# Reading page numbers ahead, unrolling the rotary-key loads and moving the second sample group between the heads of a latent-attention step

## The chip, the core and the metric

The kernel runs on one core of one Trainium2 chip. The metric is the time of one execution on the device in microseconds. Three runs of the kernel before gave 940.86 us as their median (938.93 to 948.01). Engines are named as the profile names them: PE is TensorE (matmuls), DVE is VectorE, ACT is ScalarE, POOL is GpSimd, and SP is SyncE, which computes nothing and issues most of the transfers.

## The reference, cut to what matters

The reference is one inference step of a decoder with two layers, for a prompt of 256 tokens and a sample group of 8 sequences with one new token each, all in float32 with a model width of 1024. Layer 0 mixes tokens with a causal convolution, layer 1 with multi-head latent attention; behind each mixer stand a mixture of 32 experts (two per token) and a gated embedding, and at the end a norm.

The change lies in the attention of layer 1. Each of the 8 sample sequences has 1024 past positions in a paged cache. A page table of 8 times 8 integers says which pages of the pool are a sequence's own:

```
def latent_attend(q_lat, q_pe, c_kv, k_pe, mask):
    s = (einsum('bqhl,bkl->bhqk', q_lat, c_kv)
         + einsum('bqhr,bkr->bhqk', q_pe, k_pe)) * ATTN_SCALE
    p = softmax(where(mask, s, -inf))
    return einsum('bhqk,bkl->bqhl', p, c_kv)

def gather_past(j):
    ckv = cache_ckv[page_table, j].reshape(n_seq, -1, KV_LORA)      # 8 x 1024 x 256
    kpe = cache_kpe[page_table, j].reshape(n_seq, -1, QK_ROPE_DIM)  # 8 x 1024 x 32
```

There are 16 heads. The prompt attends to itself with keys and values expanded per head; the samples attend in the latent space, to the cache and to their own new token.

## The kernel before, in words

The program is written by hand for each engine: five instruction streams, each in the order of its own block, and semaphores between them. Nothing reorders an engine's work, so what stands behind a wait waits as well. Matmul results go to 8 banks of PSUM taken in turn (`open_bank`); `arrive` waits until a bank's result is there, `freed` until a bank has been read out.

**Weights and the ring.** Weights come in pieces of 1 MB through a ring of 9 slots, filled by SP in a fixed order (`fill`, `load_expert`); piece g waits for the last use of piece g minus 9 (`used_up`, table `last`). Between the experts of layer 0 (`expert_stream(0)`) and those of layer 1 (`expert_stream(1)`) SP issues 16 pieces: 4 of the gated embedding (from G_PG0), 2 of the query compression (G_DQ), 2 of the key compression (G_DKV), 3 that expand the queries (G_UQ to G_UQ+2), 1 for the keys (G_UK), 1 for the values (G_UV) and 3 of the 4 of the output projection (G_WO). The last one of the output projection is issued behind the cache loads.

**Cache pages.** The 8 sample sequences are two groups of 4 (SB = 4), called group 0 and group 1. A page's latent rows are 256 KB (128 partitions, the rows and their transpose beside each other); 32 pages are one group, 8.4 MB. SP issues one transfer per page (`load_cache`, line 1933). Sequences 0 and 1 of a group go into `page0` (in the arena) and `page1` (in `xn_sq`), sequences 2 and 3 into four ring slots, free once the query expansion is through (SP waits for bank ("qn", 7)). Group 1 goes to the same places, so it waits for group 0's last use, bank ("sv", 0). Each page's number has to be in a register of the issuing engine first: `page_numbers` reads 8 of them with `value_load`, 32 for a group, and SP does so in front of each group's transfers, behind the waits for "kpe" and "kv". The rotary keys of a page are 16 KB; POOL issues their transfers in `load_kpe` (lines 1853 to 1860), 4 loops of 8 turns for a group, and each turn reads one page number (line 1857) and issues one transfer (line 1859). Group 1's rotary keys go to the place of group 0's (`KPT`), so POOL waits for bank ("ss", 0, 1), the second of the three score banks of group 0, before it begins. Between the two groups POOL issues four stores of outputs (lines 1873 to 1877).

**The heads and the sample groups.** PE runs a loop over i = 0 to 18. Step i computes the scores of head i (line 848), for odd i up to 11 the keys of two heads to come (line 483), turns the softmax weights of head i - 2 (line 856), and for even i from 4 the values of two heads (line 870). DVE and ACT run loops of the same steps (maximum, exponential, normalising, copying out). A sample group has four parts on PE: `sample_scores` (line 892, waits for the group's latent rows in `s_ckin` and rotary keys in `s_kpin`), `sample_weights` (lines 901 and 905), `sample_values` (lines 914 and 916, fills bank ("sv", B)) and `sample_out` (line 922). DVE has `sample_max`, `sample_new`, `sample_turned`, `sample_rows` and `sample_latent`, and ACT `sample_exp`. Group 0's four parts stand at the ends of PE's steps i in SAMPLE_AT = [3, 5, 7, 9]; DVE's and ACT's parts are tied to the same numbers. Group 1 stands behind the whole loop on all three engines. Behind both come the samples' values of all heads ("so", line 949) and the output projection "wo" (line 483 again), with which layer 1 goes on to its norm, its router (line 544), its experts (line 623) and the rest.

Of the kernel before, what the change touches and what calls it, by code (L numbers as in the profile page):

```python
# [17 lines left out]
TP, TS = 256, 8  # L18
# [16 lines left out]
H, DN, DR, DV = 16, 64, 32, 64  # L35
QL, KL = 384, 256
KQ, KK = QL // P, KL // P
PAGES, PAGE = 8, 128
PAST = PAGES * PAGE
SB = 4  # L40
# [32 lines left out]
UW = 288  # L73
SW = (TQ - 1) * NQ + TP
PAIRS = KD // 2
SAMPLE_AT = [3, 5, 7, 9]
HK = DN + DR


# [26 lines left out]
G_PG0 = G_MOE0 + NMOE  # L106
# [57 lines left out]
def build(nc, a, out):  # L164
    NPOOL = a["cache_ckv"].shape[0]

    with ExitStack() as ctx:
# [227 lines left out]
        def arrive(eng, key):  # L395

            b, u = taken[key]
            eng.wait_ge(full[b], u + 1)
            return bank[b]
# [59 lines left out]
        def _(pe):  # L459
# [436 lines left out]
            def sample_weights(B):  # L896
                pe.wait_ge(t_pe, B + 1)
                for hf in range(2):
                    ps = open_bank(pe, ("sp", B, hf))
                    for g in range(4):  # L900
                        t = tr(ps[:, g * P:(g + 1) * P], pp[:, (4 * hf + g) * P:(4 * hf + g + 1) * P], ident)
                    t.then_inc(is_full(("sp", B, hf)), 1)
                ps = open_bank(pe, ("sn", B))
                pe.wait_ge(t_pn, B + 1)
                tr(ps[0:TS, 0:P], pnew, ident).then_inc(is_full(("sn", B)), 1)
# [19 lines left out]
            for i in range(H + 3):  # L925
                if i < H:
                    scores(i)
                if i % 2 == 1 and i // 2 + 2 < KD:
                    keys(i // 2 + 2)
                if i == 1:  # L930
                    turn_queries()
                if 2 <= i < H + 2:
                    turn_weights(i - 2)
                if i >= 4 and i % 2 == 0:
                    values(i // 2 - 2)

                if i in SAMPLE_AT:
                    (sample_scores, sample_weights, sample_values, sample_out)[SAMPLE_AT.index(i)](0)
            sample_scores(1)
            sample_weights(1)  # L940
            sample_values(1)
            sample_out(1)
            ps = open_bank(pe, "so")
            for B in range(TS // SB):
                freed(pe, ("st", B))
# [26 lines left out]
        def _(dve):  # L972
# [549 lines left out]
            for i in range(H + 2):  # L1522
                if i < H:
                    head_max(i)
                if 1 <= i <= H:
                    head_norm(i - 1)
                if i == 1:
                    queries_in()
                if i >= 5 and i % 2 == 1:
                    head_out((i - 5) // 2)  # L1530
                if i == SAMPLE_AT[1]:
                    sample_new(0)
                if i - 1 in SAMPLE_AT:
                    (sample_max, sample_turned, sample_rows, sample_latent)[SAMPLE_AT.index(i - 1)](0)
            for c in range(KD):
                if (H + 1 - 5) // 2 < c:
                    head_out(c)
            sample_max(1)
            sample_new(1)
            sample_turned(1)  # L1540
            sample_rows(1)
            sample_latent(1)
            ps = arrive(dve, "so")
            v.tensor_copy(oT[:, :, TP:T], ps[:, 0:KD * TS].rearrange("p (c b) -> p c b", c=KD))\
# [10 lines left out]
        def _(act):  # L1555
# [227 lines left out]
            for i in range(H + 2):  # L1783
                if i % 2 == 1 and i // 2 + 2 < KD:
                    keys_in(i // 2 + 2)
                if i < H:
                    head_exp(i)
                if i >= 2:
                    head_weights(i - 2)
                if i == SAMPLE_AT[0] + 1:  # L1790
                    sample_exp(0)
            sample_exp(1)
            squares("n4", hT, KD, h_ready(("wo",)))
            root("n4")
            act.wait_ge(s_done, 32 + 64)
# [12 lines left out]
        def _(pool):  # L1808
# [41 lines left out]
                                           expert_weights(l, e, c)).then_inc(x_w[l], 16)  # L1850
                        pool.wait_ge(x_dn[l], w + 1)

            def load_kpe(B):

                for i in range(SB):
                    with pool.Fori(0, PAGES) as n:  # L1856
                        pg = pool.value_load(pages[0:1, bass.ds(n + (SB * B + i) * PAGES, 1)], min_val=0,  # L1857
                                             max_val=NPOOL - 1)
                        pool.dma_start(KPT[DR * i:DR * (i + 1), bass.ds(n * PAGE, PAGE)],  # L1859
                                       a["cache_kpeT"][bass.ds(pg, 1)].rearrange("o p f -> p (o f)"))\  # L1860
                            .then_inc(s_kpin, 16)

            moe(0)
            pool.wait_ge(s_add, KD * NGR)
            pool.wait_ge(s_pg, 16)
            pool.dma_start(wukT, a["ukT"]).then_inc(s_uk, 16)
            arrive(pool, "kpe")
            g.memset(qlat, 0.0).then_inc(s_qz, 1)
            g.memset(qps, 0.0).then_inc(s_qz, 1)
            g.memset(qsT[:, KD:KD + 3, :], 0.0).then_inc(s_qz, 1)  # L1870
            load_kpe(0)
            pool.wait_ge(s_ck, KK)
            pool.dma_start(out["ckv_p"], ckvT[:, :, 0:TP]).then_inc(s_done, 16)
            pool.dma_start(out["ckv_s"], ckvT[:, :, TP:T]).then_inc(s_done, 16)
# [1 line left out]
            pool.dma_start(out["kpe_p"], kpeT[0:DR, 0:TP]).then_inc(s_done, 16)  # L1876
            pool.dma_start(out["kpe_s"], kpeT[0:DR, TP:T]).then_inc(s_done, 16)
            arrive(pool, ("ss", 0, 1))
            load_kpe(1)
            moe(1)  # L1880

        @block.sync
        def _(sp):
# [93 lines left out]
                for g in range(NSLOT + 2 * p, min(NSLOT + 2 * p + 2, G_MOE0)):  # L1977
                    fill(g)
            expert_stream(0)
            for g in range(G_PG0, G_PIN1 - 1):  # L1980
                fill(g)
            sp.wait_ge(s_pg, 16)
            arrive(sp, "kpe")
            arrive(sp, "kv")
            for B in range(TS // SB):
                numbers = [page_numbers(SB * B + i) for i in range(SB)]
                for i in range(SB):
                    load_cache(SB * B + i, numbers[i])
            for g in range(G_PIN1 - 1, G_MOE1):
                fill(g)  # L1990
            expert_stream(1)
# [94 lines left out]
```

## Time and profile before

| | us |
|---|---|
| median of three runs | 940.86 |
| the three runs | 938.93, 940.86, 948.01 |
| the profiled execution's own time | 949.18 |
| its span in the profile | 947.2 |
| PE busy | 783.3 (83% of the span) |
| PE weight load busy | 566.7 (60%) |
| DVE busy | 319.4 (34%) |
| ACT busy | 206.6 (22%) |
| POOL busy | 56.0 (6%) |
| HBM read | 261.05 MB, 278 GB/s over the span |

The profiled execution took 8.3 us longer than the median of the three runs, of which the slowest took 948.01 us. Its span starts with the first instruction that the profiler shows and ends with the last. Busy shares are means over a program with stages of different kinds; in the two expert stages the transfer engines are saturated at 415 to 419 GB/s, in the attention stage neither they nor PE are busy all the time. The granted clock is TensorE's, as a share of its full 2.4 GHz.

### The profile page before, as it was taken

Reading aid. Unit: us, or ns where it says so; the run is one execution under the profiler, and the core shown is the slowest. Engines: PE = TensorE matmul, PEld = TensorE weight load, DVE = VectorE, ACT = ScalarE, POOL = GpSimd, SP = SyncE. Lnnn points to the kernel's source line nnn. Section 1 sums busy time; section 2 is a strip of 40 time slices with the busy share of each in tenths; the row PEclk is TensorE's granted clock in tenths of the full one; section 3 lists DMA queues with packets and bytes.
Section 4 is the critical chain, followed back from the end, with each engine's and each line's share of the span. In section 5 each row is a group of like instructions: output and inputs, shape, how many; then the busy total and the mean of one; then the engine's idle time right before and its main releaser. Section 6 shows DMA issues by size and latency. Waiting matters only on the chain.

```text
span 947.2 us, 16693 instructions
## 1 busy us (share of the span) xinstructions
PE 783.3 (83%) x6434; PEld 566.7 (60%) x6434; DVE 319.4 (34%) x948; ACT 206.6 (22%) x490; POOL 56.0 (6%) x95
## 2 busy tenths in 40 slices
PE   5999789998777796989997685798997687778894
PEld 4876468765544464667774362588765355445683
DVE  2332134433221331255265271226233132213435
ACT  2100132512111111132135251015311111111222
POOL 5100000000000000000033232000000000000000
PEclk9999889999988988999999796799999898899997
DMA  9853716599999999974319074468699999999501
GB/s 376 300 174 79 249 51 256 191 420 406 415 417 416 415 418 417 418 292 145 122 60 358 22 236 140 171 229 321 270 399 419 415 418 415 418 416 415 225 1 46
DMA packets 59613, 269.32 MB, mean 284 GB/s; under 512 B 7312, under 2 KB 12704, under 8 KB 38416
## 3 DMA queue, kind: packets, MB, share of 16 engines
q1 hardware_dynamic: 53232, 259.37, 69.0%
q10 hardware_dynamic: 3712, 5.35, 1.9%
q0 software_dynamic: 2592, 3.54, 1.3%
q8 instruction: 53, 0.87, 0.4%
q14 instruction: 24, 0.20, 0.1%
HBM read 261.05 MB, written 2.52 MB: 278 GB/s over the span
## 4 chain that ended last, share of the span: by engine, by line
PE 53%; DMA 23%; issue 13%; POOLq 4%; DVE 3%; ACT 1%; ACTq 1%; POOL 1%; SPq 0%; DVEq 0%
DMA ring<-in_moe_w_up 22%; PE bank L483 16%; PE bank L623 15%; PE bank L602 5%; POOLq L1857 3%; PE bank L649 3%; PE bank L664 3%; PE bank L507 3%; PE bank L892 2%; DMA ring<-in_stream 1%; PE bank L558 1%; PE bank L544 1%; PE bank L467 1%; POOLq L1859 1%; POOLq L1856 1%
## 5 line engine op out<-in xcount | busy, mean ns | idle before, releaser
L623 PE MATMUL bank<-ring,arena 128*32 128x256 f32 x2048 | 148.1, 436 | 63.5 <-DMA ring<-in_moe_w_up 61.2
L623 PEld LDWEIGHTS bank<-ring,arena 128*32 128x32 f32 x2048 | 86.8, 125 | 130.3 <-issue 108.1
L483 PE MATMUL bank<-xn_sq,ring 128*128 128x264 f32 x480 | 110.3, 392 | 10.9 <-DMA ring<-in_stream 10.9
L483 PE MATMUL bank<-arena,ring 128*128 128x264 f32 (+1 forms) x456 | 109.6, 401 | 6.5 <-ACT arena L1597 4.0
L483 PEld LDWEIGHTS bank<-xn_sq,ring 128*128 128x128 f32 x480 | 92.5, 193 | 27.8 <-issue 11.7
L1229 DVE TENSOR_TENSOR arena<-arena,bank 128x128 f32<-128x128 f32 x34 | 9.8, 288 | 288.4 <-ACT arena L1638 288.4
L483 PEld LDWEIGHTS bank<-arena,ring 128*128 128x128 f32 x456 | 90.3, 199 | 23.7 <-issue 7.0
L602 PEld LDWEIGHTS bank<-arena 128*128 128x128 f32 x864 | 97.9, 192 | 9.4 <-issue 9.4
L602 PE MATMUL bank<-arena 128*128 128x128 f32 (+1 forms) x864 | 101.1, 277 | 2.0 <-DVE arena L1199 2.0
L649 PE MATMUL bank<-ring,arena 128*32 128x512 f32 x512 | 65.4, 598 | 16.6 <-ACT arena L1645 16.5
L664 PE MATMUL bank<-arena 128*128 128x264 f32 (+1 forms) x288 | 70.5, 399 | 4.7 <-ACT arena L1654 4.7
L664 PEld LDWEIGHTS bank<-arena 128*128 128x128 f32 (+1 forms) x288 | 54.0, 192 | 21.3 <-ACT arena L1654 6.9
L1246 DVE TENSOR_TENSOR hT<-hT,bank 128x264 f32<-128x264 f32 x144 | 61.7, 429 | 13.3 <-PE bank L664 11.1
L1654 ACT COPY arena<-bank 64x512 f32<-64x512 f32 x68 | 39.4, 580 | 76.6 <-PE bank L649 75.8
L1638 ACT ACTIVATE arena<-bank 128x128 f32<-128x128 f32 x34 | 9.4, 277 | 166.5 <-PE bank L623 166.5
L649 PEld LDWEIGHTS bank<-ring,arena 128*32 128x32 f32 x512 | 14.9, 109 | 44.3 <-ACT arena L1645 24.3
L1859 POOL DMA_DIRECT2D arena<-in_cache_kpeT x64 | 32.1, 501 | 71.9 <-issue 71.9
L507 PE MATMUL bank<-arena 128*32 128x256 f32 x512 | 31.3, 406 | 4.5 <-DMA arena<-arena 4.5
L1565 ACT ACTIVATE xn_sq<-hT 128x264 f32<-128x264 f32 x40 | 16.1, 420 | 74.3 <-DVE hT L1000 66.6
L892 PE MATMUL bank<-arena 128*32 128x512 f32 (+1 forms) x96 | 15.4, 468 | 19.7 <-DMA arena<-in_cache_kpeT 19.7
L1630 ACT COPY arena<-bank 128x512 f32<-128x512 f32 (+1 forms) x18 | 10.1, 561 | 94.1 <-PE bank L602 94.1
L507 PEld LDWEIGHTS bank<-arena 128*32 128x32 f32 x512 | 17.0, 117 | 18.3 <-DMA arena<-arena 4.9
(243 smaller groups left out, 790.2 us busy)
## 6 DMA issues: line engine op xcount, KB each, us to landing
ring<-in_moe_w_gate SPq DMA_DIRECT2D x60, 1024.0 KB, 14.0
ring<-in_moe_w_up SPq DMA_DIRECT2D x60, 1024.0 KB, 10.7
ring<-in_moe_w_down SPq DMA_DIRECT2D x60, 1024.0 KB, 12.9
ring<-in_stream SPq DMA_DIRECT2D x35, 1024.0 KB, 12.5
ring<-in_cache_ckv SPq DMA_DIRECT2D x32, 256.0 KB, 7.6
arena<-in_moe_w_down SPq DMA_DIRECT2D x4, 1024.0 KB, 13.3
arena<-in_cache_ckv SPq DMA_DIRECT2D x16, 256.0 KB, 4.1
xn_sq<-in_cache_ckv SPq DMA_DIRECT2D x16, 256.0 KB, 5.5
```

What stands on the lines that cost most here:

```text
L483: t = mm(ps[:, 0:cols], lhs(k), rhs(k), start=(k == 0), stop=(k == n - 1))
L507: t = mm(ps[CG * b:CG * (b + 1), 0:TP], dg[:, c, TQ * b + q, :], shifted[p % 2][:, b, c % 2, NQ * q:NQ * q + TP], start=(q == 0), stop=(q ...
L602: t = mm(bank[k // 4][:, (k % 4) * n:(k % 4 + 1) * n], XR[:, i, k * P:(k + 1) * P], S[:, j % 2, i, 0:n], start=(i == 0), stop=(i == 2))
L623: t = mm(bank[2 + r][p0:p0 + U, 0:F].rearrange("p (c f) -> p c f", c=2), x, w[i][:, :, k * F + c * P:k * F + (c + 1) * P], start=(k == 0), ...
L649: t = mm(bank[4 + r][p0:p0 + U, :], hidT[:, r, U * (2 * i + c):U * (2 * i + c + 1)], w[i][:, c, h * 512:(h + 1) * 512], start=(c == 0), st ...
L664: mm(bank[CBANK[k % 4]][:, 0:T], O[0:n, j % 2, k * P:(k + 1) * P], gate[0:n, j % 2, :], start=True, stop=True).then_inc(s_cb, 1)
L892: t = mm(ps[HP * i:HP * (i + 1), 0:n], qlat[:, k, b, :] if k < KK else qps[:, b, :], keys, start=(k == 0), stop=(k == KK))
L1246: v.tensor_tensor(hT[:, k, :], hT[:, k, :], bank[CBANK[k % 4]][:, 0:T], ALU.add).then_inc(s_add, 1)
L1565: s.activation(sq[:, at + k, :], src[:, k, :], ACT.Square).then_inc(s_sq, 1)
L1654: s.copy(O[64 * r:64 * r + 64, j % 2, 512 * h:512 * (h + 1)], bank[4 + r][64 * h:64 * h + 64, :])\
L1857: pg = pool.value_load(pages[0:1, bass.ds(n + (SB * B + i) * PAGES, 1)], min_val=0, max_val=NPOOL - 1)
L1859: pool.dma_start(KPT[DR * i:DR * (i + 1), bass.ds(n * PAGE, PAGE)], a["cache_kpeT"][bass.ds(pg, 1)].rearrange("o p f -> p (o f)"))\
```

## The change

Four things are changed, and nothing of what is computed.

1. `SAMPLE_AT` holds a list for each group: group 0 at steps 2, 4, 6, 8 (one step earlier), group 1 at steps 12, 14, 16, 18 instead of behind the loop. DVE's and ACT's parts follow; `sample_latent(1)` alone still stands behind DVE's loop.
2. SP reads group 0's 32 page numbers between the pieces G_UQ and G_UQ+1 of the ring, and group 1's right behind the issue of group 0's transfers.
3. POOL reads group 0's 32 page numbers behind layer 0's experts, in front of its wait for their sums, and group 1's behind the issue of group 0's rotary keys, in front of the four stores.
4. POOL issues the rotary keys of a group as 32 transfers written out, with the numbers in registers, instead of 4 loops of 8 turns.

```diff
-SAMPLE_AT = [3, 5, 7, 9]
+SAMPLE_AT = [[2, 4, 6, 8], [12, 14, 16, 18]]
@@ PE
-                if i in SAMPLE_AT:
-                    (sample_scores, sample_weights, sample_values, sample_out)[SAMPLE_AT.index(i)](0)
-            sample_scores(1)
-            sample_weights(1)
-            sample_values(1)
-            sample_out(1)
+                for B in range(TS // SB):
+                    if i in SAMPLE_AT[B]:
+                        (sample_scores, sample_weights, sample_values, sample_out)[SAMPLE_AT[B].index(i)](B)
@@ DVE
-                if i == SAMPLE_AT[1]:
-                    sample_new(0)
-                if i - 1 in SAMPLE_AT:
-                    (sample_max, sample_turned, sample_rows, sample_latent)[SAMPLE_AT.index(i - 1)](0)
+                for B in range(TS // SB):
+                    if i == SAMPLE_AT[B][1]:
+                        sample_new(B)
+                    if i - 1 in SAMPLE_AT[B]:
+                        (sample_max, sample_turned, sample_rows, sample_latent)[SAMPLE_AT[B].index(i - 1)](B)
...
-            sample_max(1)
-            sample_new(1)
-            sample_turned(1)
-            sample_rows(1)
             sample_latent(1)
@@ ACT
-                if i == SAMPLE_AT[0] + 1:
-                    sample_exp(0)
-            sample_exp(1)
+                for B in range(TS // SB):
+                    if i == SAMPLE_AT[B][0] + 1:
+                        sample_exp(B)
@@ POOL
-            def load_kpe(B):
+            def page_numbers(B):
+                return [[pool.value_load(pages[0:1, b * PAGES + n:b * PAGES + n + 1], min_val=0, max_val=NPOOL - 1)
+                         for n in range(PAGES)] for b in range(SB * B, SB * (B + 1))]
+
+            def load_kpe(numbers):
                 for i in range(SB):
-                    with pool.Fori(0, PAGES) as n:
-                        pg = pool.value_load(pages[0:1, bass.ds(n + (SB * B + i) * PAGES, 1)], min_val=0,
-                                             max_val=NPOOL - 1)
-                        pool.dma_start(KPT[DR * i:DR * (i + 1), bass.ds(n * PAGE, PAGE)],
-                                       a["cache_kpeT"][bass.ds(pg, 1)].rearrange("o p f -> p (o f)"))\
+                    for n in range(PAGES):
+                        pool.dma_start(KPT[DR * i:DR * (i + 1), n * PAGE:(n + 1) * PAGE],
+                                       a["cache_kpeT"][bass.ds(numbers[i][n], 1)].rearrange("o p f -> p (o f)"))\
                             .then_inc(s_kpin, 16)
             moe(0)
+            pool.wait_ge(s_pg, 16)
+            numbers = page_numbers(0)
             pool.wait_ge(s_add, KD * NGR)
-            pool.wait_ge(s_pg, 16)
             pool.dma_start(wukT, a["ukT"]).then_inc(s_uk, 16)
             arrive(pool, "kpe")
...
-            load_kpe(0)
+            load_kpe(numbers)
+            numbers = page_numbers(1)
             pool.wait_ge(s_ck, KK)
...
             arrive(pool, ("ss", 0, 1))
-            load_kpe(1)
+            load_kpe(numbers)
@@ SP
-            for g in range(G_PG0, G_PIN1 - 1):
+            for g in range(G_PG0, G_UQ + 1):
                 fill(g)
             sp.wait_ge(s_pg, 16)
+            numbers = [page_numbers(i) for i in range(SB)]
+            for g in range(G_UQ + 1, G_PIN1 - 1):
+                fill(g)
             arrive(sp, "kpe")
             arrive(sp, "kv")
             for B in range(TS // SB):
-                numbers = [page_numbers(SB * B + i) for i in range(SB)]
                 for i in range(SB):
                     load_cache(SB * B + i, numbers[i])
+                if B == 0:
+                    numbers = [page_numbers(SB + i) for i in range(SB)]
```

## Rows read from the trace of the kernel before

**Rows 1.** Chain of waits, 480 to 680 us: start, duration, what it went through.
```profile
524.30 1.75 DMA arena<-in_cache_kpeT
526.30 7.67 PE bank L892 x48
...
582.55 1.82 DMA arena<-in_cache_kpeT
584.62 7.53 PE bank L892 x48
...
604.70 0.49 DVE rstd L1510
...
608.58 30.45 PE bank L483 x128
```

**Rows 2.** Timeline of PE: start, duration, instruction, idle before and releaser.
```profile
475.40 2.39 PE L467 MATMUL bank<-xn_sq,cst 128*128 128x264 f32 x10
...
495.20 2.83 PE L483 MATMUL bank<-arena,ring 128*128 128x264 f32 x12
...
512.70 0.52 PE L856 MATMUL bank<-cst,arena 128*128 128x128 f32 x3 [0.49 <-DVE arena L1467]
...
515.00 0.52 PE L856 MATMUL bank<-cst,arena 128*128 128x128 f32 x3 [0.26 <-DVE arena L1467]
...
551.36 0.92 PE L848 MATMUL bank<-arena 96*128 96x128 f32 x4
...
574.15 1.55 PE L870 MATMUL bank<-arena 128*64 128x128 f32 x12 [0.66 <-ACT arena L1767]
```

**Rows 3.** Timeline of POOL, the issues of the rotary keys and the stores.
```profile
477.10 0.52 POOL L1859 DMA_DIRECT2D arena<-in_cache_kpeT  x1 [0.64 <-issue]
...
524.30 0.50 POOL L1859 DMA_DIRECT2D arena<-in_cache_kpeT  x1 [1.01 <-issue]
...
526.65 0.73 POOL L1877 DMA_DIRECT2D out_kpe_s<-arena  x1
535.43 0.50 POOL L1859 DMA_DIRECT2D arena<-in_cache_kpeT  x1 [8.05 <-issue]
```

**Rows 4.** Chain of waits, 503 to 506.5 us, one turn of POOL's loop.
```profile
503.37 0.30 POOLq L1857
...
503.93 0.08 POOLq L1859
...
504.07 0.50 issue
```

**Rows 5.** Timeline of SP's queue: start, length of the stretch, transfers issued.
```profile
401.48 9.22 SPq L1919 DMA_DIRECT2D ring<-in_stream  x4
...
426.35 0.33 SPq L1919 DMA_DIRECT2D ring<-in_stream  x1
...
495.51 4.72 SPq L1933 DMA_DIRECT2D arena<-in_cache_ckv  x8
...
504.71 8.14 SPq L1933 DMA_DIRECT2D ring<-in_cache_ckv  x16
551.61 4.06 SPq L1933 DMA_DIRECT2D arena<-in_cache_ckv  x8
```

**Rows 6.** Stretches: length, busy time of each engine, granted clock, DMA share, GB/s.
```profile
520.00:521.00 1.00, 0.00 (x0) 0.00 (x0) 0.00 (x0) 0.00 (x0) 0.26 (x1) 0.50 0.82 293
...
526.30:534.00 7.70, 7.70 (x72) 2.37 (x72) 0.00 (x0) 0.00 (x0) 1.08 (x3) 0.70 0.12 34
...
577.00:578.00 1.00, 0.00 (x0) 0.00 (x0) 0.00 (x0) 0.00 (x0) 0.00 (x0) 0.50 0.23 78
```

**Rows 7.** Transfers of the rotary keys: duration ns min/median/max on POOL, and landing.
```profile
L1859 POOL DMA_DIRECT2D arena<-in_cache_kpeT x64: 496/496/608, 477.1 to 582.6; - x64
...
DMA to landing us min/median/max: 1.7/3.2/5.5
```

**Rows 8.** Chain of waits, 700 us to the end: the first long transfer waits.
```profile
714.00 9.58 DMA ring<-in_moe_w_up
```

## The prediction

> **What bounds the kernel now.** I began with the chain of waits through the attention stage. The reader is to see that it runs over POOL twice: PE's sample scores start when the last rotary-key transfer of a group has landed, at 526.30 us for group 0 and at 584.62 us for group 1, and the output projection starts at 608.58 us [rows 1]. PE's own timeline says how long it had been ready: its step 3 ends at 515.52, so it stood still for 10.8 us, and its last head work ends at 575.70, so it stood still for 8.9 us [rows 2]. Then the timelines of the two issuing engines. POOL issues group 0's rotary keys from 477.10 to 524.30, 31 intervals of 1.52 us [rows 3], though the transfer instruction itself takes 0.50 us. SP issues group 0's latent rows only from 495.51 [rows 5], though what it waited for (the sums of squares) was over at 475.40 + 2.39 = 477.8 [rows 2]; in the 17.7 us between it reads 32 page numbers, 0.55 us each. Last the stretches of the transfer engines: after those 32 transfers they are busy until about 521, after group 1's until about 577.5 [rows 6]. So the rotary keys end both waits by 3 to 7 us over the latent rows, and what comes behind them is the second group's serial tail, 584.6 to 608.6, in which PE has no heads to do.
>
> Behind the projection the order is fixed by PE until 714, where the expert stream begins to hold it [rows 8]. The stream's pieces wait for ring slots that PE frees in the projection and after, and for the router's order, so I let everything behind "wo" move with its start, one for one.
>
> **SP, group 0.** The page numbers are read behind piece G_UQ, issued at about 410.4, the last of four [rows 5]. 32 x 0.55 = 17.7 us end at 428.4; the piece that follows was issued at 426.35 [rows 5], so it comes 2 us later. Its user is the query expansion after 480 us; the cover is 50 us, and the cost nothing. The first 16 pages then start at 477.8 instead of 495.5. The other 16 wait for the last query bank, full at 495.20 + 2.83 = 498.0 [rows 2]; their issue takes 8.1 us [rows 5]. Landing: 32 pages took from 495.5 to 521, 25.5 us. Sixteen take at least half, 12.8 us, and at most the 8.1 us of issue and the 8 us from the last issue (504.71 + 8.14 = 512.85) to 521 [rows 5, 6]: 510.8 to 514.1. I take 512, as the first half is out of the way by then.
>
> **POOL, group 0.** Reading a number took 503.37 to 503.93, 0.56 us; the address 0.14 us; the issue 0.50 us; the other 0.3 us of a turn are the loop [rows 4]. Reading moves in front of POOL's wait for the sums of layer 0's experts; its 18 us lie beside the last experts, and only the keys' wait at 477 would show them. It costs nothing. Written out, a transfer takes 0.14 + 0.50 = 0.64 to 0.7 us; the last key transfer and the four stores, which stand written out, come 0.59 us apart (524.30 to 526.65) [rows 3]. The bounds are 0.59 and 1.52; I take 0.67, near the rows of the same shape. The 32 are issued by 477.1 + 31 x 0.67 = 497.9 and land up to 5.5 us later [rows 7], at 503.4. They no longer end the wait.
>
> **PE, group 0.** Its scores now stand behind step 2, whose end is 512.70 + 0.52 = 513.2 [rows 2]. DVE's copy of the turned queries ends about then. I take a start of 513.5, 12.8 us earlier (bounds 513.2 and 514.5). They took 7.7 us at a mean granted clock of 0.70 [rows 6], having started at 1.2 GHz after the idle stretch. Without that stretch they need 7.7 x 0.70 = 5.4 us at 2.4 GHz if the clock were all; between 5.4 and 7.7 I take 6.0, near the lower, since PE is busy right up to them. End: 519.5. From there to the end of group 0's values PE does four steps: 526.30 + 7.67 = 533.97 to 551.36, 17.4 us [rows 1, 2]. The four steps of after (3 to 6) have two key chunks and two values like those (4 to 7), so again 17.4: 536.9. Up to this point 14.5 us are gained.
>
> **POOL, group 1.** 32 readings end at 498.6 + 32 x 0.56 = 516.5, the four stores at about 519; the wait for the second score bank ends near 518.5. The cover for the readings is thus just long enough, and if it fell short by 5 us nothing would change: 32 transfers of 0.67 us end at 540.5 and land by 546, 17 us before they are needed (below).
>
> **SP, group 1.** The readings (506.2 to 524) lie under PE's steps; cover 13 us. The transfers start 0.25 us after group 0's values (551.36 to 551.61) and landed 577.5 - 551.6 = 25.9 us later [rows 2, 5, 6]: 536.9 + 0.25 + 25.9 = 563.0. This is the wait that is late next.
>
> **PE, group 1.** Eleven steps from 551.36 to 575.70 are 2.2 us each [rows 2]; six steps bring PE to the end of step 12 at about 550.5. It then stands for 12 us, and with it heads 13 to 15, which are queued behind the wait in order; DVE and ACT have nothing to do in the meantime. As the clock falls in such a stretch, the scores take 7.7 us again: 570.7. Steps 13 to 16 correspond to the 17.4 us, less two key chunks and the scores of a head that doesn't exist; I take 16.0 (bounds 13 and 19, the upper because group 1's work on DVE now queues with the heads'): 586.7. Steps 17 and 18 put one turning and one pair of values ahead of `sample_out`: 2.0 us (bounds 0.5 and 3.1). The rest of the tail, 604.70 to 608.58, is 3.9 us [rows 1]. The projection starts at 592.6.
>
> **Sum.** 608.6 - 592.6 = 16.0 us. The parts: 12.8 + 1.7 before group 0's values, and behind them 0.25 + 25.9 + 7.7 + 16.0 + 5.9 = 55.7 against 57.2 before, 1.5. Against the profiled execution's own 949.2 that gives 933.2 us. This execution was 8.3 us above the median of the three runs; the terms are waits and issues and don't depend on that, so I take them off the median: 940.9 - 16.0 = 924.9, say 925.
>
> **Rivals.**
> *More is gained.* Steps 13 to 18 at their lower bounds (13 + 0.5) and the group's transfers in 23 us: 4.5 + 2.9 more, 917.5. For it: PE has few waits left in heads with no keys to expand. Against: DVE's and ACT's round trip set the 2.2 us.
>
> *Half is gained.* The second half of group 0's pages takes as long as a whole group did because the rotary keys' many small packets share the engines with them: 498 + 22 = 520. Then group 0 starts at 520, 6.5 us later than forecast, at 1.2 GHz and once more 7.7 us long: 16.0 - 6.5 - 1.7 = 7.8 gained, 933. For it: landing of rotary keys stretches from 1.7 to 5.5 us beside the rows [rows 7]. Against: in the forecast the keys are all issued by 498.
>
> *The stream absorbs it.* If the experts' transfers from 714 us on [rows 8] were limited by when their stream began and that didn't move, nothing would be left: 941. Against: its pieces wait for PE's slots.
>
> *Slower: POOL can't issue faster.* The 1.52 us could be what a POOL transfer costs when 32 of them follow each other, whatever stands between. The second group would then decide: reading 32 numbers and the stores (about 21 us) would come between the two sets of transfers. With p us each, group 1's keys land at 477 + 32p + 21 + 32p + 3; with p = 1.52 at 598, PE's scores start there instead of 563, and the projection at 598 + 7.7 + 16 + 5.9 = 627.6, 19 us later than now: 960. It turns slower where the scores start after 579 (592.6 + 16.0 taken back), that is at p = 1.22. For it: no row shows more than five POOL transfers in a row without a loop. Against: those five come 0.59 us apart, and every one of the 64 lasts 0.50 us, at most 0.61 [rows 3, 7].
> The Trainium skill (SBUF — State Buffer, "SBUF: two separate sides") speaks for this rival: POOL's transfer descriptors are written through a port pair that certain DVE copies lock, and a transfer then waits for the copy. By its figures (about 620 ns alone, 3100 ns overlapped) an estimate for each transfer beside such a copy would lie far above 1.22 us. The trace doesn't agree so far: the second 32 were issued while DVE worked on the heads (535 to 576 us), and the longest of all 64 took 0.61 us [rows 7].
>
> **Chances.** Forecast 0.62, with a range of its own of 919 to 931; more 0.10; half 0.14; absorbed 0.06; slower 0.08. About 1%, 9.4 us, is what a measurement of this kernel can tell from no change. Faster by over that: the forecast, more, and half of "half", 0.79. Within: the other half and the absorbed case, 0.13. Slower 0.08. The range takes in the forecast's bounds, "more" in part and "half": 916 to 935.
>
> **What would show it.** In the trace of after: SP's first page at about 478 and its seventeenth at 498; POOL's rotary keys 0.6 to 0.7 us apart; group 0's scores near 513.5 at a high clock, ended by a DVE copy or latent rows and no more by rotary keys; one wait of about 12 us at line 892 near 551 to 563, now on latent rows; "wo" near 592. The prediction is wrong if POOL's intervals stay above 1.2 us, if PE's wait for group 1 is longer than 20 us, if steps 13 to 18 take more than 25 us, or if "wo" moves and the first expert wait near 714 doesn't.

## The result and the profile after

The changed kernel took 932.5 us, the median of 20 runs (925.16 to 938.57), against 945.8 us for 20 runs of the kernel before (938.93 to 954.67). The ratio is 0.987 with a 95% interval of 0.9846 to 0.9893: 10 to 15 us faster. The time lies in the forecast range of 916 to 935 us, though above the 919 to 931 that the forecast had without its rivals; the forecast gain of 16.0 us is a little above the interval.

The profiled execution took 925.16 us, 24.0 less than the 949.18 of before. That is more than the change did, and one has to cut the trace to see it. The query expansion (36 matmuls on line 483), ahead of which PE's code is the same and SP's and POOL's readings are hidden, starts 8.7 us earlier, at 471.72 instead of 480.44 us; in the other traces of this study it starts between 476.6 and 482.8. So I compare **the stretch** from that start to the start of the output projection: 608.58 - 480.44 = 128.1 us before, 588.00 - 471.72 = 116.3 us after, and the same 116.3 in a second profile of the changed kernel. The change is worth 11.9 us there. Each kernel was profiled once and only the changed one twice, so the stretch of one trace is a single reading. Behind the projection 3.4 us differ, of which more below. To set a moment of after beside one of before, add 8.7 us.

The chain of waits of the changed kernel, 470 to 620 us (start, duration, what it went through):

```profile
471.72 26.63 PE bank L483 x104
...
504.60 5.52 PE bank L892 x69
...
523.62 3.59 PE bank L914 x64
527.21 0.64 PE bank L916 x2
528.01 0.34 SPq L1932
...
545.67 8.06 DMA ring<-in_cache_ckv
553.72 0.35 issue
554.08 8.23 PE bank L892 x69
562.30 0.87 PE bank L848 x4
...
576.37 5.42 PE bank L914 x64
581.79 0.62 PE bank L916 x2
...
588.00 31.57 PE bank L483 x128
```

POOL is gone from it, where before it stood twice [rows 1]. Group 0's scores (504.60) follow PE's step 2 with no wait, and do 5.5 us of work, not 7.7 [rows 6]. The one wait left is for latent rows: from the end of group 0's values (527.85) over SP's 32 issues to the landing at 553.7. Behind it, from 562.30 to 582.41, comes what the forecast had too short.

PE's waits, 500 to 620 us (who waited for whom: us in total, times, longest):

```profile
PE bank L892 <- DMA ring<-in_cache_ckv: 11.3, 1, 11.3
PE bank L856 <- DVE arena L1464: 3.8, 7, 1.5
PE bank L870 <- ACT arena L1761: 3.0, 6, 0.7
PE bank L901 <- ACT arena L1775: 2.3, 1, 2.3
```

POOL's timeline, which answers to [rows 3]:

```profile
467.68 7.93 POOL L1856 DMA_DIRECT2D arena<-in_cache_kpeT  x14
476.00 10.34 POOL L1856 DMA_DIRECT2D arena<-in_cache_kpeT  x18 [0.39 <-issue]
504.09 0.70 POOL L1872 DMA_DIRECT2D out_ckv_p<-arena  x1 [17.75 <-issue]
...
505.78 0.73 POOL L1876 DMA_DIRECT2D out_kpe_s<-arena  x1
510.65 18.37 POOL L1856 DMA_DIRECT2D arena<-in_cache_kpeT  x32 [4.13 <-PE bank L892]
```

32 transfers take 18.37 us, 0.574 each instead of 1.52. The 17.75 us in front of the stores are the 32 readings, 0.555 each; behind the stores POOL still waits 4.1 us for group 0's scores, so the readings are hidden.

SP's queue, which answers to [rows 5]:

```profile
469.29 4.35 SPq L1932 DMA_DIRECT2D arena<-in_cache_ckv  x8
473.82 4.49 SPq L1932 DMA_DIRECT2D xn_sq<-in_cache_ckv  x8
489.47 8.78 SPq L1932 DMA_DIRECT2D ring<-in_cache_ckv  x16
528.01 3.95 SPq L1932 DMA_DIRECT2D arena<-in_cache_ckv  x8
```

With 8.7 added the first page goes out at 478.0 and the seventeenth at 498.2. The transfer engines are done with group 0 in the microsecond from 503 (busy share 0.26, and nothing from 504 to 505), about 512 on the scale of before as forecast, and only 1 us ahead of PE's scores: an earlier place for group 0 would soon wait for latent rows. And POOL's transfers of the rotary keys, which answer to [rows 7] (ns min/median/max):

```profile
L1856 POOL DMA_DIRECT2D arena<-in_cache_kpeT x64: 496/496/748, 467.7 to 528.5; - x64
...
DMA to landing us min/median/max: 1.7/2.2/5.6
```

Issued nearly three times as densely, half of them still take 496 ns, and the longest 748. That longest one met DVE's copy of the keys' rotary part, from SBUF to SBUF (POOL's transfers, 477.2 to 477.7 us, and DVE's timeline):

```profile
L1856 POOL DMA_DIRECT2D arena<-in_cache_kpeT x1: 748/748/748, 477.2 to 477.2; - x1
```

```profile
477.38 0.75 DVE L1416 COPY arena<-arena 32x512 f32<-32x512 f32 x2
```

### The profile page after: what moved, and what is told of

Read it like the earlier page. It is cut to its first block, busy times and chain, and to the rows that moved or that the text cites. A ratio compares the mean times of both kernels' runs of the same rounds, so it can differ in the third digit from the quotient of the medians.

```text
span 923.2 us, 16491 instructions
## 1 busy us (share of the span) xinstructions
PE 767.7 (83%) x6434; PEld 558.3 (60%) x6434; DVE 318.5 (35%) x948; ACT 205.8 (22%) x490; POOL 56.1 (6%) x95
## 4 chain that ended last, share of the span: by engine, by line
PE 64%; DMA 25%; DVE 4%; issue 2%; ACT 2%; SPq 2%; ACTq 1%; DVEq 0%
PE bank L483 25%; DMA ring<-in_moe_w_up 23%; PE bank L623 15%; PE bank L602 6%; PE bank L649 3%; PE bank L664 2%; PE bank L507 2%; SPq L1932 1%; PE bank L892 1%; DMA ring<-in_stream 1%; PE bank L914 1%; PE bank L467 1%; PE bank L544 1%; DMA ring<-in_cache_ckv 1%; PE bank L745 1%
## 5 line engine op out<-in xcount | busy, mean ns | idle before, releaser
L623 PE MATMUL bank<-ring,arena 128*32 128x256 f32 x2048 | 143.2, 424 | 67.7 <-DMA ring<-in_moe_w_up 65.3
L623 PEld LDWEIGHTS bank<-ring,arena 128*32 128x32 f32 x2048 | 83.7, 122 | 132.9 <-issue 109.0
L1243 DVE TENSOR_TENSOR hT<-hT,bank 128x264 f32<-128x264 f32 x144 | 61.7, 428 | 12.9 <-PE bank L664 10.8
L649 PEld LDWEIGHTS bank<-ring,arena 128*32 128x32 f32 x512 | 14.8, 109 | 44.3 <-ACT arena L1639 24.3
L1624 ACT COPY arena<-bank 128x512 f32<-128x512 f32 (+1 forms) x18 | 10.1, 562 | 94.1 <-PE bank L602 94.1
L507 PE MATMUL bank<-arena 128*32 128x256 f32 x512 | 28.5, 380 | 1.5 <-DMA arena<-arena 1.5
L1218 DVE COPY arena<-bank 128x512 f32<-128x512 f32 (+1 forms) x18 | 11.9, 661 | 36.9 <-PE bank L602 36.9
L507 PEld LDWEIGHTS bank<-arena 128*32 128x32 f32 x512 | 16.2, 110 | 13.3 <-DMA arena<-arena 1.9
## 6 DMA issues: line engine op xcount, KB each, us to landing
ring<-in_moe_w_down SPq DMA_DIRECT2D x60, 1024.0 KB, 13.3
```

Of the source, the lines that this page charges most:

```text
L507: t = mm(ps[CG * b:CG * (b + 1), 0:TP], dg[:, c, TQ * b + q, :], shifted[p % 2][:, b, c % 2, NQ * q:NQ * q + TP], start=(q == 0), stop=(q ...
L623: t = mm(bank[2 + r][p0:p0 + U, 0:F].rearrange("p (c f) -> p c f", c=2), x, w[i][:, :, k * F + c * P:k * F + (c + 1) * P], start=(k == 0), ...
L649: t = mm(bank[4 + r][p0:p0 + U, :], hidT[:, r, U * (2 * i + c):U * (2 * i + c + 1)], w[i][:, c, h * 512:(h + 1) * 512], start=(c == 0), st ...
L1218: v.tensor_copy(xe[:, j % 2, 0:4, 0:n], bank[0][:, 0:4 * n].rearrange("p (k n) -> p k n", k=4))\
L1243: v.tensor_tensor(hT[:, k, :], hT[:, k, :], bank[CBANK[k % 4]][:, 0:T], ALU.add).then_inc(s_add, 1)
L1624: s.copy(xe[:, j % 2, 4:KD, 0:n], bank[1][:, 0:4 * n].rearrange("p (k n) -> p k n", k=4))\
```

## Experiments

**The changed kernel again, and its parts taken apart.** First the changed kernel without an edit (after_again):

> The changed kernel once more, beside the others of this group on the same chip. I follow one stretch in every trace: from the start of the query expansion (line 483, 36 matmuls) to the start of the output projection. It was 608.58 - 480.44 = 128.1 us before and 588.00 - 471.72 = 116.3 us after. Expected: 116 to 117 us, and 0.987 of the kernel before.

Measured: stretch 594.64 - 478.29 = 116.35 us, ratio 0.9863 [0.983, 0.9895]. The stretch repeats to 0.1 us, although the profiled executions differ by 6 us in all.

The places of both groups without the rest (t_move_only, SP's and POOL's blocks as before):

```diff
-SAMPLE_AT = [3, 5, 7, 9]
+SAMPLE_AT = [[2, 4, 6, 8], [12, 14, 16, 18]]
...
```

> The new places of both groups alone; SP and POOL read and issue as before. The stretch from the query expansion to the output projection is what I compare: 128.1 us before, 116.3 us after. Theory 1 (the issuing engines' earlier and faster work made the gain, the place of group 1 costs): group 0's scores still wait for the rotary keys to about 526 us of the old trace, group 1's keys still land at about 584.5 (POOL's 1.52 us each), and behind them come 8.2 + 20.2 + 5.6 us instead of 24: stretch of 136 to 139 us, 8 to 10 us longer than before, ratio about 1.01. Theory 2 (the interleaving gains by itself): 120 to 128 us, ratio below 1.

Measured: stretch 616.30 - 479.55 = 136.75 us, ratio 1.0102 [1.0034, 1.0171]. Chain of waits, 470 to 660 us:

```profile
523.44 1.92 DMA arena<-in_cache_kpeT
525.61 6.95 PE bank L892 x48
581.16 1.86 DMA arena<-in_cache_kpeT
583.26 7.26 PE bank L892 x69
...
616.30 31.04 PE bank L483 x128
```

The rotary keys end both waits as before. The new places alone make the kernel slower: PE now stands 17.3 us at step 12 with heads behind it.

POOL as before, the rest changed (t_pool_before):

```diff
-            numbers = page_numbers(0)
...
-                    for n in range(PAGES):
+                    with pool.Fori(0, PAGES) as n:
+                        pg = pool.value_load(...)
...
```

> The change with POOL as before (4 loops of 8 turns, numbers read inside), SP reading ahead and the groups at their new places. Theory 1: POOL's keys end both waits, so SP's part shows nothing and the stretch is that of the places alone, 136 to 139 us. Rival (SP's earlier rows were half of the gain): 124 to 130 us.

Measured: stretch 614.64 - 476.91 = 137.7 us, ratio 1.0097 [1.0062, 1.0132], the same as the places alone. SP sends its first page 2.4 us before the query expansion starts (474.48), and nothing waits for it.

SP as before, the rest changed (t_sp_before):

```diff
-            numbers = [page_numbers(i) for i in range(SB)]
             for g in range(G_UQ + 1, G_PIN1 - 1):
...
             for B in range(TS // SB):
+                numbers = [page_numbers(SB * B + i) for i in range(SB)]
```

> The change with SP as before (page numbers read in front of group 0's transfers, behind the waits), POOL and the places as changed. Theory 1: group 0's rows land at 521 of the old trace, its scores start 8 us later than in the changed kernel and at 1.2 GHz, and all behind them moves with it: stretch of 125 to 128 us, that is 9 to 11 us of the change's gain gone. Rival (SP's reading is hidden elsewhere): 116 to 118 us.

Measured: stretch 610.14 - 482.78 = 127.4 us, ratio 0.9971 [0.9933, 1.001]. PE's waits, 480 to 620 us:

```profile
PE bank L892 <- DMA ring<-in_cache_ckv: 21.3, 2, 12.2
```

Both waits are now on latent rows. With the places given (136.8 us), POOL's part alone is worth 9.4 us and SP's alone nothing; together they are worth 20.4. PE's two waits at line 892 say why: 30.6 us in all with the places alone, 30.5 with SP's part, 21.3 with POOL's, 11.3 with both. Each part alone leaves PE waiting for the other queue's transfers.

The loop and the reading taken apart on POOL (t_inline):

```diff
                 for i in range(SB):
                     for n in range(PAGES):
+                        pg = pool.value_load(pages[0:1, b * PAGES + n:b * PAGES + n + 1], ...)
```

> The change with POOL's 64 transfers written out but each number read right in front of its transfer. It parts the loop from the reading: the changed kernel issues every 0.574 us, a reading took 0.56 us, so 1.13 us each if they add. Group 0's keys are then issued by 477.1 + 31 x 1.13 = 512 of the old trace and land at 514 to 517, group 1's at about 559, before the rows at 562.5. Stretch of 117 to 120 us. If the reading goes beside the issue, 0.6 us each and 116.3 us; if the pace stays at 1.5 us, the loop was free and the stretch is 130 us or more.

Measured: stretch 597.79 - 480.14 = 117.65 us, ratio 0.9882 [0.9812, 0.9952]. POOL's timeline, 460 to 600 us:

```profile
479.21 0.50 POOL L1859 DMA_DIRECT2D arena<-in_cache_kpeT  x1 [0.64 <-issue]
480.34 0.50 POOL L1859 DMA_DIRECT2D arena<-in_cache_kpeT  x1 [0.63 <-issue]
```

1.13 us each: of the 1.52 us, 0.39 were the loop (the difference), 0.56 the reading and 0.57 the transfer, and the last two add up to the 1.13. Writing out the loop with the numbers read in place costs the stretch only 1.3 us against reading ahead, because at 1.13 us the keys land about when PE arrives.

**Where group 1 stands.** The part of the change that cost. Group 1 behind the loop on PE, DVE and ACT, all else as changed (t_behind):

```diff
-SAMPLE_AT = [[2, 4, 6, 8], [12, 14, 16, 18]]
+SAMPLE_AT = [[2, 4, 6, 8], [99, 99, 99, 99]]
...
+            sample_scores(1)
+            sample_weights(1)
+            sample_values(1)
+            sample_out(1)
             ps = open_bank(pe, "so")
```

> Everything of the change but the place of group 1: it stands behind the head loop on PE, DVE and ACT again, group 0 stays at steps 2, 4, 6, 8. Theory 1 (heads 13 to 15 are queued behind a wait of 11 us that they could fill, and afterwards they compete with group 1's own chain): PE does steps 13 to 18 in the 11 us, starts group 1's scores within 2 us of the latent rows' landing, and needs the 24 us of the kernel before from there to the projection: stretch of 104 to 108 us, 8 to 12 us shorter than after, ratio to before about 0.976. Theory 2 (the place of group 1 is what the gain came from, since it fills its chain with head work): the serial tail costs as much as it saves, 115 to 119 us, ratio 0.985 to 0.99.

Measured: stretch 583.65 - 477.87 = 105.8 us, 10.6 less than the change; ratio 0.9772 [0.974, 0.9804], 926.7 us beside 933.4 for the changed kernel on the same chip. PE's timeline, 546 to 584 us:

```profile
559.06 0.88 PE L870 MATMUL bank<-arena 128*64 128x128 f32 x12 [0.66 <-ACT arena L1769]
560.34 0.59 PE L892 MATMUL bank<-arena 128*32 128x512 f32 x1 [0.40 <-DMA ring<-in_cache_ckv]
```

The heads fill the wait to within 0.4 us. The intervals of the two ratios to before don't touch, and theory 1 holds: heads 13 to 15 were queued behind a transfer that they don't need.

Both groups where they stood before (t_ahead_only), with the reading ahead and the unrolled issue (group 0 at steps 3, 5, 7, 9, group 1 behind the loop; the edit is the one above with the other list):

> The reading ahead on SP and POOL and the unrolled issue, with both groups where they stood before (group 0 at steps 3, 5, 7, 9, group 1 behind the loop). Theory 1: nearly all of the gain is here and more than the whole change has: group 0 starts some 2.3 us later than with step 2, group 1's rows land 2.3 us later, about when PE is through with the heads: stretch of 105 to 110 us, ratio to before 0.977 to 0.98. Theory 2 (the new places bring the gain): 120 us or more, ratio above 0.99.

Measured: stretch 584.57 - 476.60 = 108.0 us, ratio 0.9801 [0.9772, 0.9829]. So parts 2 to 4 of the change make more than the whole gain, and group 0's earlier place adds 2.2 us to them in these two traces, though the medians (926.7 and 928.2 us) don't part. Group 1's place takes 10.6 away.

Group 1 at the last steps (t_late):

```diff
-SAMPLE_AT = [[2, 4, 6, 8], [12, 14, 16, 18]]
+SAMPLE_AT = [[2, 4, 6, 8], [15, 16, 17, 18]]
...
```

In this kernel and the next, DVE's parts for group 1 also change order: `sample_new` follows `sample_max`, and the last parts stand around the last `head_out`.

> The changed kernel with group 1 at steps 15, 16, 17, 18 instead of 12, 14, 16, 18, group 0 at 2, 4, 6, 8 as changed. Theory 1: PE reaches the end of step 15 about 6 us before the rows, waits that long with two turnings and two pairs of values left: stretch of 107 to 110 us, between the 105.8 of group 1 behind the loop and the 116.3 of the change. If the head work queued behind the wait doesn't matter, it stays at 114 to 116 us.

Measured: stretch 583.35 - 478.56 = 104.8 us, shorter than the 107 to 110 us expected; ratio 0.9801 [0.976, 0.9841]. PE did wait 5.8 us and began the scores at 1.2 GHz (8.0 us). But from the scores' end at 569.1 to the values' end at 579.3 it took only 10.1 us: a turning and a pair of values stand in the wait for the weights, another turning ahead of the values, and line 914 took 3.66 us.

Group 0's values a step earlier and group 1 at steps 16, 17, 18 and behind (t_fill):

```diff
-SAMPLE_AT = [[2, 4, 6, 8], [12, 14, 16, 18]]
+SAMPLE_AT = [[2, 4, 5, 7], [16, 17, 18, 99]]
...
```

> The reading ahead and the unrolled issue, group 0 at steps 2, 4, 5, 7 (its values a step earlier than in the change, so that group 1's rows start earlier), group 1 at steps 16, 17, 18 and its last part behind the loop. Theory 1 (heads 13 to 15 must not be queued behind the wait, but a little head work fills the gaps in group 1's chain): the rows land at about the moment at which PE reaches the end of step 16, no wait above 2 us at line 892 for group 1, stretch of 102 to 105 us against 105.8 with group 1 wholly behind the loop. Theory 2 (the place within the last steps makes no difference once the wait is filled): 105 to 107 us.

Measured: stretch 586.06 - 479.51 = 106.6 us, ratio 0.9804 [0.9765, 0.9844]. The wait at line 892 for group 1 was short (0.5 us) as theory 1 has it, but the stretch is theory 2's. PE's waits, 500 to 545 us:

```profile
PE bank L914 <- DVE wdw L1501: 2.8, 1, 2.8
```

Group 0's values were issued a step earlier but waited 2.8 us for DVE's copies of the weights, which stand behind a head's maximum and norm there. They ended 56.5 us into the stretch against 56.1 in the changed kernel, so the rows didn't come earlier either (in t_fill_warm below, with the same code up to there, 54.8). Between this and the two kernels before it the measured ratios don't part.

**The clock.** Spare matmuls in the wait of group 1's scores (t_warm; their results are overwritten by the scores):

```diff
+WARM = 12
...
+                first = open_bank(pe, ("ss", B, 0))
+                if B:
+                    for _ in range(WARM):
+                        mm(first[:, 0:512], ident, cst[:, 0:512], start=True, stop=True)
                 for i in range(SB):
                     pe.wait_ge(s_ckin[i], 16 * PAGES * (B + 1))
...
```

> The changed kernel, and in front of the wait of group 1's scores 12 matmuls of 512 columns into the bank that the scores then overwrite (about 10.5 us of PE work at 2.4 GHz in a wait of 11.3 us). Theory 1a (the clock that fell in the wait is behind the long steps 12 to 16): scores in 5.5 us instead of 8.2, and the steps after them at 17 instead of 20.2 us: stretch of 110 to 112 us. Theory 1b (the queue of work on DVE and ACT is behind them, the clock falls again for lack of PE work between 562 and 570 us): only the scores get shorter, 113 to 114 us.

Measured: stretch 591.12 - 477.13 = 114.0 us, ratio 0.9833 [0.9803, 0.9863]. The scores took 5.5 us instead of 8.2, but steps 13 to 16 still 19.8 us (565.27 to 585.09): theory 1b. The clock stayed at 2.4 GHz through the spare work and the scores (granted clock 1.00 from 548 to 570) and fell behind them (0.75 from 570 to 574). The medians of this kernel and the changed one (931.1 and 933.4 us) don't part.

The same, with spare matmuls ahead of the turnings of steps 13 to 15 and of group 1's weights as well (t_warm_all):

```diff
             def turn_weights(h, warm):
                 ps = open_bank(pe, ("pt", h))
+                for _ in range(warm):
+                    mm(ps[:, 0:512], ident, cst[:, 0:512], start=True, stop=True)
...
```

> The changed kernel with the 12 spare matmuls in the wait of group 1's scores, and one more (512 columns, 0.88 us) ahead of each of the turnings of steps 13 to 15 and two ahead of group 1's weights. It parts the two halves of the long steps 13 to 16: Theory 1 (the fallen clock costs 3 of their 20 us, the round trip over DVE and ACT the rest): 16.5 to 18 us from the end of the scores to the end of the values, stretch of 110.5 to 112.5 us. Rival (the round trip alone): 19 to 21 us, stretch of 113.5 to 116 us.

Measured: stretch 590.85 - 478.62 = 112.2 us, ratio 0.9881 [0.9827, 0.9935]. Stretches of this kernel (length, busy time of PE, its weight load, DVE, ACT and POOL, granted clock, DMA share, GB/s), and below them those of the changed kernel for the same work:

```profile
566.00:570.00 4.00, 4.00 (x47) 2.65 (x40) 2.33 (x8) 1.17 (x5) 0.00 (x0) 1.00 0.00 0
570.00:574.00 4.00, 3.10 (x20) 1.70 (x19) 3.53 (x14) 2.61 (x11) 0.00 (x0) 1.00 0.00 0
574.00:578.00 4.00, 3.11 (x19) 2.16 (x18) 1.92 (x7) 1.45 (x6) 0.00 (x0) 1.00 0.00 0
```

```profile
562.30:566.00 3.70, 2.44 (x18) 1.76 (x18) 2.73 (x9) 1.35 (x5) 0.00 (x0) 1.00 0.00 0
566.00:570.00 4.00, 1.70 (x19) 1.46 (x20) 3.13 (x13) 2.83 (x12) 0.00 (x0) 0.98 0.00 0
570.00:574.00 4.00, 2.56 (x10) 1.79 (x10) 1.92 (x7) 1.05 (x4) 0.00 (x0) 0.50 0.00 0
574.00:578.00 4.00, 3.98 (x31) 2.43 (x35) 2.69 (x8) 1.08 (x4) 0.00 (x0) 0.50 0.00 0
```

At 2.4 GHz throughout, steps 13 to 16 took 17.5 us (566.70 to 584.19) instead of 20.1; in the seven traces that have these places and no spare matmuls behind the scores they took 19.7 to 20.1. So about 2.6 us of them are the clock, which had fallen to 1.2 GHz at 570 behind a stretch in which PE worked 1.70 of 4 us. The 17.5 us aren't PE's work either: 4.4 of them are the five spare matmuls of 0.88 us, and 2.3 us PE stood idle, at waits for DVE and ACT. That leaves about 10.8 us of work. The runs don't show the gain: 0.9881 is no better than the changed kernel's 0.987.

Spare matmuls in t_fill, 3, 1, 1 and 1 in the waits of its tail (t_fill_warm):

```diff
             def sample_weights(B):
+                first = open_bank(pe, ("sp", B, 0))
+                if B:
+                    for _ in range(3):
+                        mm(first[:, 0:512], ident, cst[:, 0:512], start=True, stop=True)
                 pe.wait_ge(t_pe, B + 1)
...
```

> The kernel with group 0 at 2, 4, 5, 7 and group 1 at 16, 17, 18, behind, and spare matmuls into banks that are overwritten afterwards, in PE's waits of group 1's tail: 3 of 512 columns ahead of the weights, 1 ahead of the values, 1 of 256 ahead of the last part and 1 ahead of the output of the samples (0.88 us for 512 columns). Theory: the tail runs at 2.4 GHz instead of 1.2 for half of it (values in 3.6 instead of 5.4 us, weights in 1.3 instead of 2.0, line of the samples' output 2.1 instead of 3.5): 2 to 4 us off the stretch of the same kernel without them. Rival: the spare matmuls outlast the waits and cost what they save, 0 us, or 1 to 2 us more.

Measured: stretch 582.61 - 480.50 = 102.1 us, 4.4 less than without them; ratio 0.9769 [0.9724, 0.9815], 921.8 us beside 923.5 without. Chain of waits, 470 to 660 us, of t_fill and then of this kernel:

```profile
563.04 7.68 PE bank L892 x48
```

```profile
561.75 6.42 PE bank L892 x48
```

The first spare matmul stands behind these scores. They ended 91.2 us into the stretch in t_fill and 87.7 here, with the same code up to there: 3.5 of the 4.4 us were there before any spare work, and the two traces differ by only 0.9 us behind them. Their gain isn't shown, by the trace or by the medians. The 3.5 us also say how far the stretches of two single traces can differ by themselves, so the order among t_behind, t_ahead_only, t_late, t_fill and this one stays open. Against t_behind's 0.9772 the times of whole runs don't separate the two. Both beat the kernel before and the changed one.

## Why the prediction was right, and where it was off

Moments of after below are the old trace's, 8.7 us added.

- **What bounds** was right. Both of the old waits were POOL's, and SP's rows stood close behind: with only one of the two issuing engines changed (t_sp_before, t_pool_before) little or nothing is left of the gain.
- **SP, group 0**: forecast 478 and 498, measured 478.0 and 498.2. The readings behind G_UQ cost nothing that the trace shows.
- **POOL**: forecast 0.67 us for each transfer between bounds of 0.59 and 1.52, measured 0.574, just below the lower bound. The rival that POOL can't issue faster fell with it. The Trainium skill (SBUF — State Buffer, "SBUF: two separate sides") says that POOL's transfer descriptors are written through a port pair that certain DVE copies lock, and that such a transfer waits for the copy. The trace agrees, at a size that doesn't matter here: the issue that met DVE's copy took 748 ns instead of 496. The prediction's reading that the trace of before doesn't agree was wrong: it looked at the second 32 transfers, while the same copy at 486.11 met one of the first 32, which took 583 ns.
- **PE, group 0**: start forecast 513.5, measured 513.3; length 6.0, measured 5.5; end of the values 536.9, measured 536.6.
- **SP, group 1**: forecast landing 563.0, start of the scores measured 562.8. The late wait was named and sized right (12 us forecast, 11.3 measured).
- **What comes behind**: forecast to move one for one with the projection. The first long transfer wait of the experts came at 692.88, with 8.7 added 701.6 instead of 714.00: 12.4 us earlier, beside 11.9 for the projection. The rival that the stream absorbs the gain fell. Chain of waits, 585 us on:

```profile
692.88 10.57 DMA ring<-in_moe_w_up
```

- **PE, group 1** is the term that was mis-sized. "Steps 13 to 16 correspond to the 17.4 us, less two key chunks and the scores of a head that doesn't exist; I take 16.0" was 20.1, outside my bounds of 13 and 19. Two mistakes went the same way, as the stretches of before (steps 4 to 7) and of after (steps 13 to 16) show:

```profile
534.00:551.36 17.36, 15.14 (x148) 10.74 (x138) 11.06 (x37) 8.77 (x31) 5.47 (x11) 0.90 0.05 11
```

```profile
562.30:582.41 20.11, 15.08 (x126) 9.50 (x125) 10.47 (x35) 6.30 (x23) 0.00 (x0) 0.75 0.00 0
```

I took PE's missing work off and let nothing come for it, but PE stood idle for 5.0 us instead of 2.2, at waits for DVE and ACT. And I forecast the fallen clock for the scores but not for what follows them: at a mean granted clock of 0.75 instead of 0.90 PE was busy as long with less work. At full clock the steps took 17.5 us (t_warm_all), of which about 10.8 are PE's own work. The scores took 8.2 instead of 7.7, the tail 5.6 instead of 5.9.
- **Sum**: 16.0 forecast, 11.9 measured in the stretch. The missing 4.1 us are these 20.1 - 16.0; the other terms are off by 0.5 us or less and cancel. The medians say 945.8 - 932.5 = 13.3.
- **The absolute number** was right partly by luck: three runs of before gave 940.9, twenty gave 945.8. The 925 forecast counted from the lower median; from the later one it would have been 929.8.
- **A thing not asked.** The prediction costed group 1's new place only as a wait of 12 us with "heads 13 to 15 queued behind", and let it stand. The same rows show that those heads need about those 12 us (2.2 us a step, six steps). Working out the change without that part would have shown a better kernel: t_behind is 10.6 us shorter in the stretch.

## What to carry to other kernels

When two queues feed one wait, look up the second-latest arrival before pricing the removal of the latest: here one engine's speed-up alone was worth 9 us, the other's nothing, and both together 20. In an engine's fixed order, put a part that waits for a transfer behind the work that doesn't need it, not in the midst of it (10.6 us here); whether a little other work among a dependent chain pays once its data has arrived isn't shown, as t_late and t_behind don't part. And where an engine waits in a stretch for round trips over other engines, don't take missing work off its length in full.

## What the runs showed of the hardware

A page number read with `value_load` costs 0.555 us on POOL, as on SP (0.55), and doesn't overlap the transfer's issue on the same engine (1.13 us for both in t_inline).

In each of the fourteen traces one POOL transfer issue meets DVE's copy from SBUF to SBUF of 32 x 512 elements, twice (0.75 us). It took 743 to 753 ns in the ten in which POOL's transfers follow each other directly, and 576 to 668 in the four others, while the issues on either side of it took 496 or 498.

The time behind the projection isn't constant either, although its code is the same. It was 338.6 us in the trace of before (947.2 - 608.58), 335.2 and 334.6 in the two of the changed kernel, 334.7 in t_fill, and 342.0 and 342.2 in t_behind and t_ahead_only. Chains of waits, behind the projection, of the changed kernel and of t_behind:

```profile
622.52 4.11 PE bank L544 x48
```

```profile
616.87 7.08 PE bank L544 x48
```

The router's 48 small matmuls took 4.1 us in one and 7.1 in the other. PE comes to them, and to four matmuls ahead of them, out of a wait of 1.8 us. In the changed kernel the clock stays at 2.4 GHz through them; in t_behind it fell to 1.2 GHz as they began (stretches):

```profile
616.00:617.00 1.00, 1.00 (x8) 0.87 (x7) 0.10 (x1) 0.13 (x1) 0.00 (x0) 1.00 1.07 442
618.00:619.00 1.00, 1.00 (x6) 1.00 (x7) 1.00 (x1) 0.00 (x0) 0.00 (x0) 0.50 1.00 418
```

In the five traces in which I found them above 6 us (t_behind, t_ahead_only, t_late, t_fill_warm, t_warm_all) the part behind the projection was 339.6 to 342.2 us; in the nine with 4.1 us (all others) it was 334.6 to 339.9. The 24 matmuls that follow them (line 558) part these nine once more: 2.8 us in after, after_again, t_sp_before and t_fill, with 334.6 to 335.2 us behind the projection, and 4.5 us in before, t_move_only, t_pool_before, t_inline and t_warm, with 337.4 to 339.9, the clock falling a few microseconds later (granted clock 0.75 from 646 to 648 in before). Together the two lines differ by 4.3 us between after and t_behind; the rest of the 6.8 us isn't taken apart. Each kernel was profiled once (the changed one twice), so whether a place of group 1 brings it about or it falls out by chance stays open. It goes the way in which the medians (6.7 us between the change and t_behind) fall short of the stretches (10.6 us).
